# A fused three-layer model on one core: tile 0's transposes placed inside tile 1's last weight matmuls, and norm products, a split and the output's stores cut in halves

## What is computed

```
for i in (0, 1):                                   # first block
    x = x + 0.5 * swiglu_ffn(rms_norm(x, ffn1_norm[i]), ffn1_w_in[i], ffn1_w_out[i])   # width 2816
    h = rms_norm(x, mix_norm[i])
    x = x + (pool_mixer(h) if i == 0 else nsa_mixer(h))
    x = x + memory_cross_attention(rms_norm(x, xattn_norm[i]), rms_norm(mem, mem_norm[i]), w_q, w_kv, w_o)
    x = x + 0.5 * swiglu_ffn(rms_norm(x, ffn2_norm[i]), ffn2_w_in[i], ffn2_w_out[i])
x = rms_norm(x, final_norm)
# second block, one layer; shift, scale and gate come from silu(c) @ ada_w + ada_b
u = rmsnorm(x, norm_mix) * (1 + scale1) + shift1   # u @ w_in feeds three attention branches and gates
x = x + gate1 * (merged_branches @ w_o)
u2 = rmsnorm(x, norm_mlp) * (1 + scale2) + shift2
x = x + gate2 * (relu(u2 @ w_ff1) ** 2 @ w_ff2)    # width 4096
out = rmsnorm(x, norm_final)

rms_norm(x, g) = x * rsqrt(mean(x * x, -1) + 1e-6) * g
```

## Time and profile before

| | |
|---|---|
| time before, three runs | 1719.08, 1719.42, 1723.54 us; median 1719.42 |
| time of the profiled run | 1717.44 us |
| its span, first to last instruction | 1715.7 us |
| mean granted TensorE clock | 0.983 of full speed |
| busy: TensorE matmul, VectorE, ScalarE, GpSimd | 1624.2, 1038.5, 753.4, 90.4 us |

### The profile page before, as it was taken

One profiled execution on the slowest core, in us unless ns is written; L12 is line 12 of the kernel. 1 busy time (PEld: TensorE's weight loads), 2 busy tenths in 40 slices (PEclk: granted clock), 3 DMA queues, 4 the chain that ended last, 5 costly groups with the idle time before them and its releaser, 6 DMA issues.

```text
span 1715.7 us, 21734 instructions
## 1 busy us (share of the span) xinstructions
PE 1624.2 (95%) x8403; PEld 1351.8 (79%) x8403; DVE 1038.5 (61%) x1323; ACT 753.4 (44%) x943; POOL 90.4 (5%) x145
## 2 busy tenths in 40 slices
PE   6999997999999999999988899999989999889997
PEld 6788876878888888888975687888778877678886
DVE  4577655567765576755567455555556775665444
ACT  4444443444434343444368444434444455344432
POOL 1000000000000000001000021000010030100000
PEclk9999998999999999999999899999999999999999
DMA  8587744288775477763350243656645531545550
GB/s 308 196 292 238 252 147 164 67 274 272 237 259 173 162 269 264 246 217 119 102 174 1 105 142 128 209 181 196 190 171 204 164 128 62 183 161 197 193 196 25
DMA packets 210201, 311.82 MB, mean 182 GB/s; under 512 B 16538, under 2 KB 145590, under 8 KB 209873
## 3 DMA queue, kind: packets, MB, share of 16 engines
q1 hardware_dynamic: 204112, 288.90, 50.2%
q0 software_dynamic: 6016, 21.94, 3.6%
HBM read 306.59 MB, written 4.21 MB: 181 GB/s over the span
## 4 chain that ended last, share of the span: by engine, by line
PE 83%; DVE 7%; ACT 4%; issue 2%; DMA 1%; PEld 1%; DVEq 1%; POOL 1%; ACTq 0%; PEldq 0%; SPq 0%; POOLq 0%
PE ps L2171 25%; PE ps L2173 25%; PE ps L2172 25%; DVE wlo L1377 2%; PE ps L2323 1%; ACT whi L773 1%; PE ps L2230 1%; PE ps L2471 1%; PE ps L2607 1%; DMA area<-in_gate_b 1%; ACT xn L1084 1%; PE ps L2448 1%; ACT xn L819 1%; DMA raw<-in_xattn_w_kv 1%; DVEq L1360 1%
## 5 line engine op out<-in xcount | busy, mean ns | idle before, releaser
L1377 DVE TENSOR_TENSOR wlo<-raw,whi 128x2048 fp32r<-128x2048 f32 x255 | 581.8, 2299 | 236.3 <-ACT whi L773 235.4
L773 ACT ACTIVATE whi<-raw 128x2048 fp32r<-128x2048 f32 x255 | 482.4, 1911 | 184.9 <-PE ps L2173 162.8
L2171 PE MATMUL ps<-wlo,aT_hi 128*128 128x512 f32 (+2 forms) x1312 | 514.5, 392 | 25.4 <-DVE aT_lo L1410 14.3
L2173 PE MATMUL ps<-whi,aT_hi 128*128 128x512 f32 (+2 forms) x1312 | 505.6, 385 | 0.0
L2172 PE MATMUL ps<-whi,aT_lo 128*128 128x512 f32 (+2 forms) x1312 | 505.4, 385 | 0.0
L2171 PEld LDWEIGHTS ps<-wlo,aT_hi 128*128 128x128 f32 x1312 | 249.0, 190 | 78.2 <-issue 21.7
L2173 PEld LDWEIGHTS ps<-whi,aT_hi 128*128 128x128 f32 x1312 | 249.0, 190 | 49.5
L2172 PEld LDWEIGHTS ps<-whi,aT_lo 128*128 128x128 f32 x1312 | 249.3, 190 | 46.7 <-issue 0.7
L2171 PE MATMUL ps<-wlo,hT_hi 128*128 128x512 f32 x480 | 187.8, 391 | 0.0
L2173 PE MATMUL ps<-whi,hT_hi 128*128 128x512 f32 x480 | 187.0, 390 | 0.0
L2172 PE MATMUL ps<-whi,hT_lo 128*128 128x512 f32 x480 | 186.8, 389 | 0.0
(11 more groups left out here) (326 smaller groups left out, 1203.6 us busy)
## 6 DMA issues: line engine op xcount, KB each, us to landing
raw<-in_ffn_w_in SPq DMA_DIRECT2D x176, 512.0 KB, 4.9
raw<-in_ffn_w_out SPq DMA_DIRECT2D x88, 512.0 KB, 4.3
raw<-in_w_ff SPq DMA_DIRECT2D x64, 512.0 KB, 4.8
raw<-in_ada_w SPq DMA_DIRECT2D x48, 512.0 KB, 5.3
raw<-in_w_in SPq DMA_DIRECT2D x48, 512.0 KB, 4.8
raw<-in_xattn_w_kv SPq DMA_DIRECT2D x32, 512.0 KB, 6.5
raw<-in_xattn_w_q SPq DMA_DIRECT2D x16, 512.0 KB, 4.7
raw<-in_xattn_w_o SPq DMA_DIRECT2D x16, 512.0 KB, 5.6
```

The source lines that it names most:

```text
L773: act.activation(to, of, ACT.Copy).then_inc(hi_ready[slot], 1)
L1377: dve.tensor_tensor(lo, of, hi, ALU.subtract).then_inc(lo_ready[slot], 1)
L2171: pe.matmul(o, lh, rl, start=start, stop=False, skip_group_check=True)
L2173: return pe.matmul(o, lh, rh, start=False, stop=stop, skip_group_check=True)
```

## The change

- Norm products, and the shift behind them, are made in halves of 512 columns. A new semaphore `cols_normed` counts first halves, `rows_normed` second ones; TensorE's first four transposes of a tile wait for the one, the other four for the other.
- At norms 4, 7, 8, 9 and 12 TensorE no longer waits for tile 0's transposes until tile 1's matmuls are done: they stand inside them. In `project` they are ahead of k = 5 of tile 1's last chunk (norms 4 and 8), of k = 2 (norm 9, with the sums moved from k = 5 to k = 1) and of k = 7 (norm 12); in layer 1's first `ffn` (norm 7) they are ahead of the last six matmuls. VectorE lowers tile 0's banks before it adds tile 1 there.
- Tile 1's transposes in the next stage come after 18 matmuls of tile 0 and not after twelve. That holds for norm 3 and `head` as well.
- At the end of each `ffn`, and of the gated `project`, VectorE splits slot 1 in two halves of 1024 columns: one ahead of tile 0's addition, one behind it.
- `head` has no matmuls on zeros, and on VectorE tile 1's addition comes behind tile 0's product.
- The output is stored in four DMAs of 128x512 and not two of 128x1024.

The diff, cut to its core (the edits to `rows`, to `query`, `nsa_inputs` and `wide_inputs`, where (0, 4) becomes (0, 6), and to `mlp`, which has the same edit as `ffn`'s `up_first`, repeat what stands here):

```diff
--- before.py
+++ after.py
@@ -140,7 +140,7 @@
-        squared, rstd_made, rows_normed = sem("squared"), sem("rstd_made"), sem("rows_normed")
+        squared, rstd_made, cols_normed, rows_normed = (sem(n) for n in ("squared", "rstd_made", "cols_normed", "rows_normed"))
@@ -536,9 +536,11 @@
             for t in range(T):
+                sp.wait_ge(cols_normed, T * (len(gains) - 2) + t + 1)
+                sp.dma_start(out[0, t * P:(t + 1) * P, 0:512], x[:, t, 0:512]).then_inc(stored, 16)
                 sp.wait_ge(rows_normed, T * (len(gains) - 1) + t + 1)
-                sp.dma_start(out[0, t * P:(t + 1) * P, :], x[:, t, :]).then_inc(stored, 16)
-            sp.wait_ge(stored, 16 * T)
+                sp.dma_start(out[0, t * P:(t + 1) * P, 512:1024], x[:, t, 512:1024]).then_inc(stored, 16)
+            sp.wait_ge(stored, 32 * T)
@@ -1364,6 +1366,15 @@
+            def split_half(slot, part):
+
+                if part == 0:
+                    dve.wait_ge(hi_ready[slot], uses.next(slot))
+                half = slice(1024 * part, 1024 * part + 1024)
+                ins = dve.tensor_tensor(wlo[:, slot, half], raw[:, slot, half], whi[:, slot, half], ALU.subtract)
+                if part:
+                    ins.then_inc(lo_ready[slot], 1)
@@ -1456,20 +1467,17 @@
+                    inside = turn and m not in (0, 3)
+                    if modulate:
+                        dve.wait_ge(mod_kept, 10)
                     for t in range(T):
+                        if t and inside:
+                            self.lower_rows(norm_banks(m), (0, 1))
                         if t:
                             self.update_rest()
-                            if turn and m:
-                                self.lower_rows(norm_banks(m), (0, 1))
-                        dve.wait_ge(rstd_made, 2 * m + t + 1)
-                        last = dve.scalar_tensor_tensor(out=to[:, t, :], in0=src[:, t, :], scalar=rstd[:, t:t + 1],
-                                                        in1=gain[:, m % 2, :], op0=ALU.mult, op1=ALU.mult)
-                        if modulate:
-
-                            step(last)
-                            dve.wait_ge(mod_kept, 10)
-                            last = dve.tensor_tensor(xn[:, t, :], xn[:, t, :], mod[:, 0:1024], ALU.add)
-                        last.then_inc(rows_normed, 1)
+                        if t and m == 3:
+                            self.lower_rows(norm_banks(m), (0, 1))
+                        self.weigh_tile(m, t, src, to, modulate)
@@ -1479,13 +1487,23 @@
+                def weigh_tile(self, m, t, src, to, modulate=False):
+
+                    dve.wait_ge(rstd_made, 2 * m + t + 1)
+                    for c, done_with in enumerate((cols_normed, rows_normed)):
+                        half = slice(512 * c, 512 * c + 512)
+                        last = dve.scalar_tensor_tensor(out=to[:, t, half], in0=src[:, t, half], scalar=rstd[:, t:t + 1],
+                                                        in1=gain[:, m % 2, half], op0=ALU.mult, op1=ALU.mult)
+                        if modulate:
+                            step(last)
+                            last = dve.tensor_tensor(xn[:, t, half], xn[:, t, half], mod[:, half], ALU.add)
+                        last.then_inc(done_with, 1)
@@ -1591,11 +1609,12 @@
-                    split(1)
+                    split_half(1, 0)
                     dve.wait_ge(half_done, halves.next())
                     add(0)
                     if last:
                         self.weigh_rows(0)
+                    split_half(1, 1)
                     self.rest = add_second
                     if mem:
@@ -1609,13 +1628,15 @@
-                    self.update_rest()
...
                         dve.wait_ge(rstd_made, 20 + 2 * (t + 1))
-                        step(dve.scalar_tensor_tensor(out=xn[:, t, :], in0=x[:, t, :], scalar=root_out[:, 2 * t + 1:2 * t + 2],
-                                                      in1=gain[:, 1, :], op0=ALU.mult, op1=ALU.mult))
-                        dve.tensor_tensor(xn[:, t, :], xn[:, t, :], mod[:, 0:1024], ALU.add).then_inc(rows_normed, 1)
+                        for c, done_with in enumerate((cols_normed, rows_normed)):
+                            half = slice(512 * c, 512 * c + 512)
+                            step(dve.scalar_tensor_tensor(out=xn[:, t, half], in0=x[:, t, half], scalar=root_out[:, 2 * t + 1:2 * t + 2],
+                                                          in1=gain[:, 1, half], op0=ALU.mult, op1=ALU.mult))
+                            dve.tensor_tensor(xn[:, t, half], xn[:, t, half], mod[:, half], ALU.add).then_inc(done_with, 1)
                         if t == 0:
+                            self.update_rest()
                             self.weigh_rows(1)
                         self.lower_rows(range(4), (2 * t, 2 * t + 1))
@@ -1725,7 +1746,10 @@
                     split(0)
-                    split(1)
+                    if gated:
+                        split_half(1, 0)
+                    else:
+                        split(1)
...
                     dve.wait_ge(half_done, halves.next())
                     add(1, 0).then_inc(x_half, 1)
+                    if gated:
+                        split_half(1, 1)
@@ -2224,6 +2250,8 @@
                     if normed is not None and b % 2 == 0:
+                        pe.wait_ge(cols_normed, normed + t + 1 - (2 if normed == 24 else 0))
+                    if normed is not None and b % 2 == 1:
                         pe.wait_ge(rows_normed, normed + t + 1)
@@ -2238,6 +2266,12 @@
+                turned = False
+
+                def turn_inside(self, m):
+
+                    self.turn_first(2 * m, norm_banks(m), m == 12)
+                    self.turned = True
@@ -2258,7 +2292,6 @@
                 def head(self):
-                    keep_clock(12, 7)
                     stages.next()
                     self.turn_first(20, range(4))
@@ -2269,14 +2302,17 @@
                     stages.next()
-                    if turn:
-                        self.turn_first(2 * m, norm_banks(m), m == 12)
+                    self.norms = m
+                    if turn and not self.turned:
+                        self.turn_first(2 * m, norm_banks(m))
+                    self.turned = False
@@ -2293,12 +2329,14 @@
-                    def up_part(i, s, t):
+                    def up_part(i, s, t, later=False):
                         pe.wait_ge(lo_ready[s], ub[s] + i + 1)
                         h, lw = (w[:, s, :].rearrange("p (k n) -> p k n", k=4) for w in (whi, wlo))
                         tok = slice(t * P, (t + 1) * P)
                         for r in range(4):
                             k = 4 * s + r
+                            if later and r == 2:
+                                self.turn_later()
                             last = parts(ps[:, 4 + t, :], aT_hi[:, k, tok], aT_lo[:, k, tok], h[:, r, :],
                                          lw[:, r, :], k == 0, k == KD - 1)
@@ -2313,9 +2351,7 @@
                             pe.wait_ge(aT_made, rows_ready + 2 * t + s + 1)
-                            up_part(0, s, t)
-                            if s == t == 0:
-                                self.turn_later()
+                            up_part(0, s, t, s == 1 and t == 0)
@@ -2328,10 +2364,12 @@
                         for c in range(2):
+                            if c and inside:
+                                self.turn_inside(self.norms + 1)
                             for k in range(2):
                                 last = parts(ps[:, 2 * t + c, :], hT_hi[:, k0 + k, tok], hT_lo[:, k0 + k, tok],
                                              h[:, k, c, :], lw[:, k, c, :], False, stop and k == 1)
@@ -2390,7 +2428,7 @@
-                    down_tile(1, 3, 2, True).then_inc(consumed[3], 1)
+                    down_tile(1, 3, 2, True, self.norms == 6).then_inc(consumed[3], 1)
@@ -2421,7 +2459,7 @@
-                    chunk(0, 512, rows(b), between={(0, 4): self.turn_later}, rows_from=c_turned.n - 4)
+                    chunk(0, 512, rows(b), between={(0, 6): self.turn_later}, rows_from=c_turned.n - 4)
@@ -2516,11 +2554,15 @@
+                    def inside():
+                        self.turn_inside(12 if gated else self.norms + 1)
+
+                    between = {(1, 1): sums, (1, 2): inside} if part == 0 else {(1, 7 if gated else 5): inside}
+                    chunk(2, 512, rows(bank()), between=between, half=half_done)
```

More of the change, by code:

```diff
@@ L1485, in rows @@
                     for t in range(T):
-                        dve.wait_ge(rstd_made, 2 * m + t + 1)
-                        dve.scalar_tensor_tensor(out=xn[:, t, :], in0=src[:, t, :], scalar=rstd[:, t:t + 1],
-                                                 in1=gain[:, m % 2, :], op0=ALU.mult, op1=ALU.mult).then_inc(rows_normed, 1)
+                        self.weigh_tile(m, t, src, xn)
```

(12 more changed lines are left out.)

## The result

The changed kernel takes 1723.19 us as a median of 20 runs (1716.2 to 1725.96), the kernel before 1719.18 beside it: a ratio of 1.0022, 95% interval 1.0014 to 1.0030. Forecast were 1715.9 and a range of 1711.8 to 1720.8. Those two took 1716.2 and 1716.3; the seven at 0.976 had a median of 1724.8. Runs of before beside the experiments have a median clock of 0.981.

What follows compares the result with a forecast made beforehand. TensorE, busy 1624.2 of 1715.7 us, bounds the kernel, so only its waits or work taken off it can be won. The terms sum to -3.5 us: 1713.9 for the profiled run, 1715.9 as a median; range 1711.8 to 1720.8.

Steps and rivals of the forecast that it cites:

- a third: Behind norm 12: the clock may fall, twelve slow matmuls costing 2.1 to 2.4 us; a third counted, +0.7.
- The third rival: The clock drops to 1.2 GHz behind stands at norms 7, 12 (twice) and in kv: 1723.6 us; chance 0.09.
- norm 7: Layer 1's first ffn: half split starts the product 1.1 us earlier, transposes move inside tile 1; -1.25 us.
- norm 12: Project: product 1.1 us earlier, transposes inside tile 1, then stands of 1.7 and 0.9 for tile 1; -1.9 us.
- first query: Norm 3 into query: VectorE leaves 1.37 us later, so TensorE's hs transposes wait; +0.8 us.
- kv: Second ffn of layer 0: tile 0's addition between slot 1's halves lengthens TensorE's stand of 0.62 us; +1.3 us.
- pool: First ffn of layer 0: the 6.0 us wait ahead of the pool stage shrinks through the half split; -1.1 us.
- head: VectorE's new order moves when it leaves and the gates' biases are ordered; -0.3 to +1.3, taken as +0.5 us.
- Norm 8: Norm 8 into query: norm 4's pattern gives -0.5, the hs chain is 0.8 late; +0.2 us in all.
- The biases' landing: Head: gates' biases are ordered when VectorE leaves; the forecast is wrong if their landing doesn't follow that.
- Output: Last store has 256 KB ahead of it, half a product already stored; 0 to 1.3 us won, taken as -0.7.
- the rule on small instructions: Fixed latency per instruction reading on-chip memory: some 0.1 us at five norms, 0.5 in all, left out of the sum.

Runs made afterwards that it cites:

- kv_whole: Changed kernel, but the memory ffn's second slot is split whole ahead of tile 0's addition, as before: 1716.0 us, 0.9989 of before.
- whole_delay_6: kv_whole with six matmuls of zeros (1.36 us of work) added in kv: 1725.5 us, 1.0036 of before.
- whole_delay_15: kv_whole with fifteen matmuls of zeros (3.4 us of work) added in kv: 1719.8 us, 1.0008 of before.
- changed_again: The changed kernel measured once more, nothing altered: 1722.4 us, 1.0025 of before.
- kv_alone: Kernel before with one part of the change, the memory ffn's second slot split in halves around tile 0's addition: 1720.2 us, 1.0016 of before.
- kv_zeros: Changed kernel with eight matmuls of zeros in kv where TensorE stands 1.88 us for the second slot: 1724.5 us, 1.0036 of before.
- kv_zeros_again: Changed kernel with its stand in kv filled by eight matmuls of zeros, measured once more: 1724.4 us, 1.0028 of before.

## Why the prediction was wrong

**The step that failed** is the clock: one term of +0.7, "a third" of one fall behind norm 12, with everything else at the level it had in the profile before. Norm 12 was innocent: its stretch from 1510 to 1530 us has a granted clock of 0.83 in before and 0.91 in the changed kernel. The forecast treated the clock of all other stages as fixed. What the runs showed in its place: the mean clock went from 0.981 to 0.978. In the first pair of profiles the clock took 4.4 us where the sum had 0.7. kv_whole, whole_delay_6 and whole_delay_15 show that this hangs on a delay of some 1.3 us ahead of stages that nobody edited. Between runs of the changed kernel at 0.983 and at 0.976 lie 8.5 us, more than all the gains in the sum together (7.0). The third rival named 1723.6 and was given 0.09. Its time is nearly the measured one, its mechanism only in part: of its falls the one behind `kv` is in the first profile and not in the second, norm 7 has none, norm 12 had one already, and filling `kv`'s stand with work didn't help.

**The waits**, term by term, forecast and profile: norm 4 -0.6, -0.4; norm 7 -1.25, -0.9; norm 9 -1.4, -1.5; norm 12 -1.9, -1.9; first query +0.8, +0.7; `kv` +1.3, +1.3; pool -1.1, -0.7; head +0.5, +0.5, which is 1.35 lost and 0.85 gained (I had -0.3 to +1.3). These mechanisms held, the stands of 0.6 and 1.07 among them, forecast as 0.7 and 1.0. Of the stands of 1.7 and 0.9 forecast for tile 1's transposes at norm 12 the first profile has none and 0.73, changed_again's 1.62 and 0.73. Head's +0.5 is partly luck: the forecast had the absence of the zeros at nothing, and it costs 0.8. The pace of 0.227 us a matmul was worked out with the 66 weight loads of the earlier trace rows, where the row has 68 matmuls; the twelve zeros of the earlier trace rows give (2.93 - 0.39) / 11 = 0.23, so no term moves.

**Norm 8**: forecast +0.2, found -0.6. The transposes of `hs` waited as the forecast said (0.52, for VectorE's copy),

```profile
996.48 1.06 PE L2470 MATMUL ps<-cst,hs 128*128 128x128 f32 x8 [0.52 <-DVE hs L1677]
```

but the delay was gone at 1013, behind a wait for ScalarE that ended no later than before. A stage on, the forecast didn't look.

**The biases' landing**: the first profile had the stand at 3.06, against 2.03 before, which by my own test ("if the gates' biases' landing doesn't follow VectorE's leaving") made the head step wrong.

```profile
1273.90 1.22 DVE L1906 TENSOR_TENSOR area<-area,ps 128x1024 f32<-128x1024 f32 x1 [6.80 <-DMA area<-in_gate_b]
```

Here the addition starts 13.05 us after VectorE's leave (1260.85). In before it is 11.97, and in the fifteen profiles of experiments 11.92 to 12.49, changed_again's 11.96 among them. So the landing does follow, and the 1.1 was this one execution's.

**Output**: forecast -0.7, found nothing. From the last product's start to the span's end it took 6.0 to 6.1 us before (1709.63 to 1715.7) and takes 6.0 now (1711.00 to 1717.0):

```profile
1711.00 1.41 DVE L1495 SCALAR_TENSOR_TENSOR x<-x,small,gain 128x512 f32<-128x512 f32 x2 [2.20 <-POOL small L565]
...
out_x<-x SPq DMA_DIRECT2D x4, 256.0 KB, 2.0
```

A 256 KB store lands in 2.0 us against 2.6 for 512 KB, but two halves of a product take 1.41, not 1.28, and the second store is issued behind the first. The Trainium skill ("DMA: Bandwidth & Descriptors", section on the anatomy of one DMA) says that a DMA's time has a fixed part and one that grows with its bytes; it gives the fit for transfers that GpSimd issues, and these are SP's. The part that grows agrees, 0.6 for the half. The fixed part does not: by the Trainium skill's 2.0 us a store of 256 KB would take an estimated 2.6, and it took 2.0. The span shows that landing alone was not the end's price.

The 0.13 us more for two halves shows at norms 4, 7, 8 and 9 too (1.41 or 1.42) and speaks for the rule on small instructions that the sum left out (the Trainium skill, "VectorE: DVE Perf Modes", section on the TRN2 errata): 0.1 was its estimate. The pair of rows that the forecast set against it compared two subtractions from PSUM with one product from on-chip memory, which can't test a price per instruction.

**What stays open**: which delays are bad, since two lengths at one place were tried, and why 1.36 us is bad for kv_whole and harmless for before. What sets the times of the falls in an execution, and whether some other trait of whole_delay_6 than its delay counts, was not tested; its figure rests on five runs. Also whether the clock at 1382 and behind the biases follows the same rule; those falls differ from profile to profile of one kernel and were not tested apart.

## What to carry to other kernels

Where TensorE is the bound, look up the mean granted clock of every run before believing a sum of waits: here the clock took 4.4 us in a pair of profiles and the waits won 3.1. Test a suspicious loss with a neutral delay of two lengths: if more work is faster, the loss is in how later stages meet the clock's falls, and one should judge an edit on several variants, not on one. Take more than one profile of a kernel whose times spread: one profile shows one of its ways. And before cutting a split in halves around something else, ask at each place that shares the code whether the next stage already waits for that split.

## What the hardware did that was not expected

- Work added made a kernel faster: kv_whole with 3.4 us of zeros has 1.0008, with 1.36 us 1.0036.
- Unchanged stages (866 to 912 us) had a granted clock of 0.89 in the profiles of before, kv_whole, whole_delay_15 and the changed kernel's first, and of 0.74 to 0.78 in those of changed_again, kv_alone, kv_zeros, kv_zeros_again and whole_delay_6; 305 or 306 against 274 to 279 matmuls in the same 46 us. The low ones are those in which the clock had fallen before TensorE ended its stand at 869 to 872 us.
- Filling the stand in `kv` with matmuls of zeros left the mean clock at 0.977, and the fall behind it (0.66 from 543 to 548 us in the changed kernel's first profile) is absent from changed_again's too, which has no zeros. In head, where the stand is longer, zeros bring the eight transposes behind it from 1.97 to 1.09 us.
